# Rotary embedding of the sparse layers: rows by halves instead of a rotation matmul

## What is computed

```
def apply_rope_2(x, cos, sin):
    half = x.shape[-1] // 2
    x1, x2 = x[..., :half], x[..., half:]
    return concatenate([x1 * cos - x2 * sin, x2 * cos + x1 * sin], axis=-1)
```

## Time and profile before

| | |
|---|---|
| median of three runs | 895.08 us (894.68 to 896.62) |
| the profiled execution | 899.25 us, of which the span from first to last instruction is 897.5 us |
| mean granted TensorE clock | 0.988 of full speed |
| busy share PE / PEld / DVE / ACT / POOL | 98 / 94 / 57 / 53 / 70 % |
| first sparse layer, `kw` chunk to last selection round | from about 568 to 651 us |
| second sparse layer, the same | from about 749 to 829 us |

### The profile page before, as it was taken

How to read it: one execution, slowest core, us unless ns; L and a number is a source line. 1 busy time by engine, 2 the same in 40 slices (tenths; PEclk the granted TensorE clock), 3 DMA queues, 4 the chain that set the end, 5 groups by cost and what they waited for, 6 DMA issues and landing times.

```text
span 897.5 us, 17103 instructions
## 1 busy us (share of the span) xinstructions
PE 879.7 (98%) x6825; PEld 844.8 (94%) x6825; DVE 509.2 (57%) x1113; ACT 473.9 (53%) x927; POOL 624.5 (70%) x360
## 2 busy tenths in 40 slices
PE   9999999999999999999999999999998999999996
PEld 7997999999999999999999999999987999999786
DVE  3413111599827857545432115878965558789664
ACT  5546656622356546544444445445667464456673
POOL 4833755555556987999998898776874778766353
PEclk9999999999999999999999999999997999999998
DMA  9625634343432564455655673654320427545201
GB/s 277 180 79 169 207 95 139 103 136 95 141 99 93 185 230 148 141 191 196 197 157 171 182 224 95 204 159 134 132 95 1 145 65 232 155 138 178 95 1 47
DMA packets 134622, 128.09 MB, mean 143 GB/s; under 512 B 6512, under 2 KB 132336, under 8 KB 134544
## 3 DMA queue, kind: packets, MB, share of 16 engines
q1 hardware_dynamic: 134064, 126.20, 45.1%
q10 hardware_dynamic: 480, 0.79, 0.3%
HBM read 125.80 MB, written 1.05 MB: 141 GB/s over the span
## 4 chain that ended last, share of the span: by engine, by line
PE 86%; POOL 4%; DVE 4%; ACT 3%; issue 2%; DMA 1%; POOLq 0%; ACTq 0%; DVEq 0%
PE PS L624 22%; PE PS L626 22%; PE PS L625 21%; PE PS L895 3%; PE PS L615 2%; PE PS L668 1%; PE PS L1038 1%; PE PS L672 1%; PE PS L669 1%; PE PS L798 1%; POOL w_lo L1209 1%; PE PS L857 1%; POOL u_t L1237 1%; DMA zoneB<-in_meta_tokens 1%; POOL u_t L1233 1%
## 5 line engine op out<-in xcount | busy, mean ns | idle before, releaser
L1209 POOL TENSOR_TENSOR w_lo<-ring,w_hi 128x1024 fp32r<-128x1024 f32 (+2 forms) x237 | 544.5, 2313 | 203.1 <-ACT w_hi L1365 192.2
L624 PE MATMUL PS<-x_hi,w_hi 128*128 128x256 f32 (+2 forms) x1442 | 424.7, 295 | 1.2 <-ACT zoneA L1348 0.6
L626 PE MATMUL PS<-x_hi,w_lo 128*128 128x256 f32 (+2 forms) x1442 | 410.8, 285 | 0.0
L625 PE MATMUL PS<-x_lo,w_hi 128*128 128x256 f32 (+2 forms) x1442 | 409.9, 284 | 0.0
L1365 ACT ACTIVATE w_hi<-ring 128x1024 fp32r<-128x1024 f32 (+1 forms) x235 | 237.6, 1015 | 73.3 <-PE PS L626 70.1
L624 PEld LDWEIGHTS PS<-x_hi,w_hi 128*128 128x128 f32 (+1 forms) x1442 | 271.8, 188 | 4.0 <-issue 1.2
L625 PEld LDWEIGHTS PS<-x_lo,w_hi 128*128 128x128 f32 (+1 forms) x1442 | 271.4, 188 | 1.4 <-issue 0.2
L626 PEld LDWEIGHTS PS<-x_hi,w_lo 128*128 128x128 f32 (+1 forms) x1442 | 271.6, 188 | 0.0
L2150 DVE SCALAR_TENSOR_TENSOR PS<-zoneA,cols,PS 128x256 f32<-128x256 f32 x240 | 98.6, 481 | 0.1
L1348 ACT ACTIVATE zoneA<-PS 128x272 f32<-128x272 f32 (+3 forms) x76 | 29.3, 386 | 105.5 <-PE PS L626 105.5
L1348 ACT ACTIVATE zoneB<-PS 128x256 f32<-128x256 f32 (+4 forms) x115 | 40.9, 378 | 70.7 <-DVE PS L2117 39.9
(11 more groups left out here) (327 smaller groups left out, 1362.8 us busy)
## 6 DMA issues: line engine op xcount, KB each, us to landing
ring<-in_w_in SPq DMA_DIRECT2D x58, 1024.0 KB, 5.4
ring<-in_w_ffn_in SPq DMA_DIRECT2D x22, 1024.0 KB, 5.1
ring<-in_w_out SPq DMA_DIRECT2D x12, 1024.0 KB, 5.0
ring<-in_w_ffn_out SPq DMA_DIRECT2D x16, 704.0 KB, 4.4
ring<-in_w_mla_o SPq DMA_DIRECT2D x4, 1024.0 KB, 5.0
ring<-in_w_hg_o SPq DMA_DIRECT2D x4, 1024.0 KB, 4.9
ring<-in_w_kv_b SPq DMA_DIRECT2D x2, 1024.0 KB, 5.4
ring<-in_w_q_b SPq DMA_DIRECT2D x2, 768.0 KB, 5.0
```

Of the source, the lines that this page charges most:

```text
L624: mm(out_, hi_w, hi_x, start=start, stop=False)
L625: mm(out_, hi_w, lo_x, start=False, stop=False)
L626: return mm(out_, lo_w, hi_x, start=False, stop=stop)
L1209: sub(lo_w, src, hi_w, ALU.subtract).then_inc(sem("w_lo"), 1)
```

## The change

Rows of `q`, `k` and `qi` chunks are laid out by halves: rows 0 to 63 hold the first halves of both heads of the chunk, rows 64 to 127 the second halves. This is done where a piece is rounded and subtracted: `half_views` gives each such piece as two parts, so ACT and POOL make two instructions of 512 elements per row in place of one of 1024. The rotated tile is then a swap of the two halves of the partitions, with the sign in a second sine table `sin2`.

- PE: all 26 `rope` products of the sparse layers go.
- ACT: a `swap` is two copies of 64 partitions. For "i" chunks it goes from PSUM to PSUM, beside one straight copy. For `q` and `k` it goes from PSUM to the SBUF tiles `q2s` and `k2s` (they lie in `ycat`), right before `take`. The `beside` copies go.
- DVE: cos and sin of "i" read PSUM as before. Cos and sin of `q` and `k` read `q2`, `k2`, `q2s` and `k2s` in SBUF. The sum of a `k` chunk is one instruction into `k2`.
- ACT parts the heads (`part_heads`): eight copies of `k2` into `k2r` with a scale of 1 or 0 per row. PE waits for them (`k_parted`) before the scores.
- `kw` is 128 columns, loaded by four DMAs of 32 columns each. The twin of the index key is moved by two DMAs in place of one.
- The tap tables: 4 taps in place of 7 in the selection, 3 more in the attention. The memset of `k2r` on POOL goes.

```
-TAPS_AT_TOP = {r: 104 + r for r in range(1, 8)}
-TAPS_AT_ATT = {3: 115, 4: 118, 5: 121, 6: 124}
+TAPS_AT_TOP = {r: 104 + (r + 1) // 2 for r in range(1, 8)}
+TAPS_AT_ATT = {1: 110, 3: 113, 4: 117, 5: 120, 6: 124}
...
+        def half_views(i):
+            views = piece_views(i)
+            if not by_halves(PIECES[i][0]):
+                return [views]
+            src = views[0].rearrange("p k (h s d) -> p s k h d", h=2, s=2)
+            hi_w, lo_w = (w.rearrange("p k (s h d) -> p s k h d", s=2, h=2) for w in views[1:])
+            return [(src[:, half], hi_w[:, half], lo_w[:, half]) for half in range(2)]
...
-                load(f"L{l}kw", w2[:, :, COL2["ki"]:COL2["ki"] + HD + HEADS], HD + HEADS)
+                free(f"L{l}kw")
+                dst = slot(f"L{l}kw")[:, 0:DC * P].rearrange("p (k n) -> p k n", k=DC)
+                for at, c0 in ((0, 0), (32, 40), (64, 32), (96, 32)):
+                    full(f"L{l}kw", sp.dma_start(dst[:, :, at:at + 32], w2[:, :, COL2["ki"] + c0:COL2["ki"] + c0 + 32]))
...
-                    rope("i", 5 * l + m, qiT[:, m - 1, q_from:L] if m else kiT[0:HD, :], 4)
...
-                    if i == 0:
-                        pe.wait_ge(sem("score"), 16 * (l + 1))
-                    out_of_psum(pe, *part(f"{T}{'q' if i < 4 else 'k'}", i % 4))
-                    rope("q", 8 * l + i, q2[:, i, q_from:L] if i < 4 else k2[:, i - 4, :], 4)
...
-                            pe.wait_ge(sem("q_roped"), 8 * l + 5 + i // 2)
+                            pe.wait_ge(sem("k_parted"), 4 * l + 1 + i // 2)
...
-            nc.gpsimd.memset(k2r[:, :, :], 0.0)
...
+                def swap(dst, src):
+                    for half in range(2):
+                        af(dst[64 * half:64 * half + 64, :], src[64 - 64 * half:P - 64 * half, :], ACT.Copy)
...
+                    if n in ("q", "k"):
+                        g = CHUNK[part(f"{T}{n}", m)]
+                        act.wait_ge(sem("chunk_done"), g + 1)
+                        if n == "q":
+                            swap(q2s[:, m, q_from:L], PS[:, BANK[g], 0:n_q])
+                        else:
+                            swap(k2s[:, m, :], PS[:, BANK[g], 0:L])
...
+                def part_heads(m):
+                    act.wait_ge(sem("q_roped"), 8 * l + 5 + m)
+                    for h in (2 * m, 2 * m + 1):
+                        ins = af(k2r[:, h, :], k2[:, m, :], ACT.Copy, scale=head_rows[h % 2])
+                    ins.then_inc(sem("k_parted"), 1)
...
-                    if i < 6:
-                        beside_q(i + 2)
                     if i == 6:
                         warm(ACT.Exp)
+                        part_heads(0)
+                    if i == 7:
+                        part_heads(1)
...
                     dsa_attention(s)
+                    if s < 2:
+                        part_heads(2 + s)
...
-            def rope_cos(i, j, rows, t0, n):
-                dve.wait_ge(sem("beside"), j + 1)
-                v.tensor_tensor(rope2_a[0:rows, i % 2, 0:n], PS[0:rows, 2 + i % 2, 0:n], cosT[0:rows, t0:t0 + n], ALU.mult)
+            def rope_cos(i, src, t0, n):
+                v.tensor_tensor(rope2_a[:, i % 2, 0:n], src, cosT[:, t0:t0 + n], ALU.mult)
+            def rope_sin(tag, i, k, src, dsts, t0, n):
+                swapped = PS[:, 4 + i % 2, 0:n]
+                v.tensor_tensor(swapped, src, sin2T[:, t0:t0 + n], ALU.mult).then_inc(sem(f"{tag}_rope_out"), 1)
                 dve.wait_ge(sem(f"{tag}_rope_out"), k + 1)
...
                 def q_cos(i):
-                    rope_cos(i, 13 * l + 5 + i, P, *((q_from, n_all) if i < 4 else (0, L)))
+                    out_of_psum(dve, *part(f"{T}{'q' if i < 4 else 'k'}", i % 4))
+                    if i < 4:
+                        rope_cos(i, q2[:, i, q_from:L], q_from, n_all)
+                    else:
+                        rope_cos(i, k2[:, i - 4, :], 0, L)
```

More of the change, by code:

```diff
@@ L99, in shape_constants @@
     put("sin", np.sin(ang).astype(np.float32))
+    put("sin2", np.where(np.arange(P)[:, None] < 64, -1.0, 1.0).astype(np.float32) * np.sin(ang).astype(np.float32))
+    put("head", (np.arange(P)[:, None] // 32 % 2 == np.arange(2)[None, :]).astype(np.float32))
     s, t = np.arange(P)[:, None], np.arange(P)[None, :]
@@ L364, in cst @@
             return const[0:rows, at:at + n]
-        ident, rotm, cosT, sinT = cst("ident"), cst("rot"), cst("cos"), cst("sin")
+        ident, rotm, cosT, sinT, sin2T = cst("ident"), cst("rot"), cst("cos"), cst("sin"), cst("sin2")
+        head_rows = [cst("head")[:, i:i + 1] for i in range(2)]
         def vec(name, c):
@@ L1341, in _, with take @@
             af = nc.scalar.activation
-            def take(name, m, dst, f=ACT.Copy, rows=P, c0=0, n=L, view=None, count=True, ahead=True, **kw):
+            def take(name, m, dst, f=ACT.Copy, rows=P, c0=0, n=L, view=None, count=True, ahead=True, first=0, **kw):
                 g = CHUNK[name, m]
                 act.wait_ge(sem("chunk_done"), g + 1)
-                src = PS[0:rows, BANK[g], PS_AT[g] + c0:PS_AT[g] + c0 + n]
+                src = PS[first:rows, BANK[g], PS_AT[g] + c0:PS_AT[g] + c0 + n]
                 ins = af(dst, view(src) if view else src, f, **kw)
@@ L1362, in round_piece @@
                 if i < len(PIECES):
-                    src, hi_w, _ = piece_views(i)
                     w_ready(act, PIECES[i][0])
-                    af(hi_w, src, ACT.Copy).then_inc(sem("w_hi"), 1)
+                    for src, hi_w, _ in half_views(i):
+                        ins = af(hi_w, src, ACT.Copy)
+                    ins.then_inc(sem("w_hi"), 1)
             def warm(f):
@@ L1635, in _, with beside_chunk @@
                         round_after(*part(f"{T}a", c))
[L1636 to L1641, removed]
+                def swap(dst, src):
+                    for half in range(2):
+                        af(dst[64 * half:64 * half + 64, :], src[64 - 64 * half:P - 64 * half, :], ACT.Copy)
+                def beside_chunk(i, name, m, n):
                     g = CHUNK[name, m]
@@ L1691, in _ @@
                         take_acc(0)
-                out_of_psum(act, *part(f"{T}k", 3))
-                act.wait_ge(sem("relu"), 16 * (l + 1))
-                for i in range(2):
-                    beside_q(i)
+                def part_heads(m):
[3 more added lines that the diff above has]
+                    ins.then_inc(sem("k_parted"), 1)
                 for i, (n, m) in enumerate(ROPE_FILL):
```

79 lines of the change are left out of this document (40 added, 39 removed).

## The result

The changed kernel took 910.83 us (median of 4 runs, 909.10 to 911.73) against 894.88 us for the kernel before (894.65 to 896.62): ratio 1.0175, 95% interval 1.0157 to 1.0193, so 16 us slower. (Two executions at a far lower granted clock, 951.54 us of the kernel before and 1424.84 us of run 2's, are left out everywhere.) Its profiled execution took 911.73 us, with a span of 909.9 us and a mean granted clock of 0.976.

What follows compares the result with a forecast made beforehand. PE was taken to lead, with DVE level in the selection. First layer +5.6, second layer +3.6 and clock +3.2 made +12.4 us on the median 895.1 us: 907.5 us, range 888 to 917 us.

Steps and rivals of the forecast that it cites:

- PE saves 12.0 us: Sparse layers: 26 rotation products at 0.46 us each go from PE, 12.0 us in all.
- index stage -2.4 and -2.1 us: Index stage: with five products gone per layer, selections start 2.4 us earlier in the first layer, 2.1 in the second.
- stay covered by PE: Index stage: ACT's work with its extra copies, some 2.4 of 3.0 us per chunk, stays hidden behind PE.
- Waits placed by hand, 10.1 and 7.7 us: Selection: DVE's cos and sin with two SBUF inputs wait for POOL's instruction, 10.1 us first layer, 7.7 second.
- the pieces up to 635.8: First layer's selection: DVE's waits behind POOL's pieces before POOL's back-to-back first taps, 5.4 us.
- Selection 33 to 35 us long: Sign to look for: DVE's selection takes 33 to 35 us, before 28.8 and 27.7 us.
- PE idle for 6 to 10 us before each first masked step: Sign to look for: PE, its chunks finished, waits 6 to 10 us for DVE before each attention's first masked step.
- Clock, 1.6 us in each attention: Attention: PE's wait brings one stretch of granted clock 0.50 per layer, 1.6 us each, 3.2 us in all.
- A difference carries over: Sum: +12.4 us on the profiled 899.25 us also holds from the runs' median, 895.1 us.
- The terms of the attention: Attention: sin 7's wait, its sum's saving of 0.4 us, and three taps, 1.2 us; to the eighth step +5.6 and +3.6.
- Gain kept: Rival: cos and sin in the selection find the port free, sum -7.8 us, 887.3 us; chance 0.18.
- Half the waits: Rival: order and pauses fall well, 9 us of waits in all, clock holds, 896 us taken; chance 0.12.

Runs made afterwards that it cites:

- run 2: Kernel before with one part of the change alone: cos of q and k reads SBUF copies, rotation products, sin and tap tables stay; 896.69 us, ratio 1.0013.
- run 1: Changed kernel with both inputs of cos and sin of q and k in PSUM again, by ACT's straight and swapped copies; 893.94 us, ratio 0.9999.
- run 10: Changed kernel with POOL's subtraction for pieces of v, zc, za and wo cut to 32 elements a row, DVE untouched; 889.93 us, ratio 0.9932.
- run 7: Changed kernel with the second query tile's mask passing its middle value through PSUM and made two steps earlier; 902.85 us, ratio 1.0099.
- run 4: Changed kernel with idle products on PE before the first masked step and after the first score of each attention; 905.50 us, ratio 1.0126.
- run 12: Kernel before with four idle products on PE in the gap at the end of the first layer's attention; 893.58 us, ratio 0.9975.
- run 5: Changed kernel with the selection's four taps moved from between cos and sin to behind the sum; 904.94 us, ratio 1.0103.
- run 8: Changed kernel, cos and sin still from SBUF, no selection taps (11 in DVE's earlier idle time), second mask through PSUM, earlier head parting; 903.17 us, ratio 1.0091.

## Why the prediction was right, and where not

The forecast was 907.5 us, range 888 to 917, slower with 0.75; measured 910.8. The mechanism is shown, by the operands (run 1: no wait in either layer) and by POOL (run 10: 0.2 us of waits in the second layer, where POOL's long instructions are gone). Step by step:

- **PE saves 12.0 us; index stage -2.4 and -2.1 us.** PE's pace of a chunk there is 3.03 us, as worked out, and DVE's of an embedding 3.13 us (forecast 3.36). The stages gained 0.9 and 1.1 us. The claim that ACT's three copies "stay covered by PE" failed at one place per layer. The bank of the first index query chunk is released only after both swap copies, and PE needs it at once, since the turned weights occupy the other one: 1.1 us of wait. Before, one copy of 0.38 us lay ahead of that release, now two of 0.37 us and a longer rounding.
- **Waits placed by hand, 10.1 and 7.7 us.** Measured 6.3 and 8.2 us. In the second layer the single waits fit as well (sin 0 forecast 2.1, measured 1.8; sin 2 2.1 and 2.0; cos 3 1.0 and 1.3), and the selection took 32.7 us, the sum of the forecast. In the first the pieces up to 635.8 cost 2.9 us, not 5.4, and the taps of POOL 2.5, not 3.0: a slip of 0.2 us in a start decides on 2 us. Cos 7 cost 0.8 us, not 1.7.
- **Selection 33 to 35 us long; PE idle for 6 to 10 us before each first masked step.** The selection took 30.9 and 32.7 us. PE was idle for 4.6 and 7.0 us, in two waits around that step.
- **The mask of the second tile.** It had no term. It cost 3.1 us and in the sum made up for most of what the first layer's waits fell short. The Trainium skill (SBUF — State Buffer, "Who interferes with whom") counts `tensor_scalar` among the operations that can take the shared port pair although they have one input. The trace agrees: 1.60 us from SBUF to SBUF beside POOL, 0.30 us with POOL nearly idle (run 10), 0.45 us into PSUM beside POOL (run 7).
- **Clock, 1.6 us in each attention.** The stretches came where expected. The second cost 0.5 us (run 4). The first cost nothing that shows up to the eighth masked step; from there to PE's gap the changed kernel took 21.4 us, and runs 1, 4 and 7, at full clock in that part, 20.1 us. So some 1.8 us in all, not 3.2. What the clock cost most had no term: from that gap to the second selection the changed kernel took 121.3 us, run 1 with full clock 115.4 us. The trace of before had most of this cost as well (121.0 us; run 12, at full clock, is 4.3 us shorter from the eighth masked step to there), so it hardly shows trace against trace, but in the medians it does.
- **"A difference carries over" to the median of the runs.** This step failed. The 4.2 us between the profiled execution of before and its median were put down to profiling and spread. They go with the half-clock stretch behind the first layer: with products in that gap no execution is near 899 us (run 12), and without them only 6 of 50 have the profiled one's mean clock, 0.988. All four of the changed kernel had 0.976 to 0.977. Trace against trace the change is +12.48 us, forecast +12.4; median against median it is +15.95. The agreement of the first pair is partly luck, as the terms above show: too much gain in the index stages (2.5 us), too little mask (3.1 us), too much wait in the first layer (3.8 us), too much clock in the attentions (1.4 us). (The terms of the attention as written add up to 5.7 and 3.7 us, not 5.6 and 3.6; that changes nothing.)
- **Rivals.** "Gain kept" (887.3 us) is near what the kernel does without most of POOL's work: 889.9 us in run 10. "Half the waits" (9 us) didn't come, with 14.5 us measured; the order decides, as run 5 (10.9 us) and run 2 (1.3 us, with cos alone) show.

What stays open: why the changed kernel met the low clock behind the first layer in its profiled execution (and, by their mean clocks, in all four), and runs 1 and 7 did not in their profiled ones. A gap of 2.1 us of PE is in all of them. Only that idle products in the gap prevent it is shown (run 12, for the kernel before).

## What to carry to other kernels

Before an operand moves from PSUM to SBUF, look what POOL does at that time: a DVE operation with two SBUF inputs costs its own 0.4 us, or up to 2.6 us where POOL has just begun a piece of 2.4 us. Where it must stay, find its place in POOL's beat: in a pause it is free, a tap ahead of it can cost 2 us, and a DVE made faster only waits longer (run 8). Copies by ACT into PSUM (three a chunk, up to 0.4 us each) buy it out, if ACT has the time: in run 1 PE waited 2.3 us in all for ACT's parting and 1.7 us for its copies out of PSUM, which stand behind them.

An operation that came free ends up in the profile as a wait of the next engine in line: before a saving on PE is counted, ask who releases its next bank.

Before a difference is carried from one trace to the median, compare the mean granted clock of that trace with those of the other executions.

## What the runs showed of the hardware

- DVE waits for the end of POOL's instruction: a sin that began 0.24 us after POOL took 2.44 us and ended 0.28 us after it, one that began 0.17 us before POOL took 0.42 us. Where DVE began first, POOL's piece grew from 2.39 to as much as 2.65 us.
- With one input in PSUM none of the 52 multiplications of run 1 waited (at most 0.45 us), beside the same POOL.
- Halving POOL's instructions raised the waits in the first layer from 6.3 to 9.8 us.
- 16 operations of the waiting form lost 1.3 us in all in one order (run 2), 32 of them 14.5 us in another (the changed kernel), with the same work on POOL.
- One gap of 2.1 us on PE can cost 4 to 5 us of execution time, but not in each execution.
